# Gathering the next group's rows later: an index-driven prefetch in a mixture-of-experts kernel, moved from the start of a group to its third chunk

## The chip, the cores and the metric

One core of a Trainium2 chip. The metric is the device time of one execution in microseconds, taken as the median of several runs; lower is better. The engines are TensorE (PE, with its weight loads as PEld), VectorE (DVE), ScalarE (ACT), GpSimd (POOL) and SyncE (SP), which here only issues transfers.

## The reference

A decoder layer on 2048 rows of width 1024: a mixer (gated linear attention and retention beside each other), then a mixture of experts. The change lies in the second part:

```
logits = h @ w_router + b_router
top_val, top_idx = top_k(logits, 4)              # 4 of 32 experts for each of 2048 rows
xs = h[rows sorted by expert]
gate, up = split(ragged_dot(xs, w_gu) + b_gu)    # w_gu: 32 x 1024 x 2048
act = (clip(up, -7, 7) + 1) * min(gate, 7) * sigmoid(1.702 * min(gate, 7))
out = ragged_dot(act, w_down) + b_down           # w_down: 32 x 1024 x 1024
y[row] += weight * out                           # then residual and a last norm
```

All of it is in float32. A product is made of three passes of TensorE over operands that are split in a high and a low part (lines 119 to 121: high by high, high by low, low by high).

## The kernel before, in words

`expert_programs` writes one program for each engine, and each runs a loop over groups (`G`). The five programs meet only through semaphores. A group is one expert with one to three tiles of 128 rows and perhaps a half tile of 64 rows (slot `HALF`); an expert with more rows gets another group, which loads the expert's weights again. These inputs give 39 groups, numbered 0 to 38 here, with 70 full tiles and 9 half tiles. `G.T` is the number of full tiles, `G.U` with the half tile, `G.nT` and `G.nU` the same of the next group, `G.before` the tiles of all groups ahead.

A group has six chunks: 0 and 2 are gate columns, 1 and 3 up columns, 4 and 5 the two halves of `w_down`. Each chunk multiplies every tile with 1024x512 weights, that is 8 steps of three matmuls for a full tile and of two for a half one. In the profile's names the weights of even chunks are `weights_first`, those of odd ones `weights_split`; the rows of the tiles lie in `weights_split` as well, the activations in `tok_a_hi` and `tok_a_lo`. So "weights_first,weights_split" is chunk 0 or 2, and "tok_a_hi" marks chunks 4 and 5.

Weights come in pieces, four to a chunk, 24 to a group, of 512 KB each, in eight buffers. SyncE issues a load (L1966) when the piece eight places earlier has been split; ScalarE makes the high part (L2073) and VectorE the low part (L2173). The same two engines split the rows (L2079, L2182) and the activations (L2097, L2270).

Rows of a tile are gathered from memory into `tok_rows` by an indirect transfer from GpSimd (L1986, 512 KB for a full tile); TensorE transposes them (L2343, `rows`). A group's first tile is transposed in the chunk 4 of the group before (`next_row`, halfway through the first tile's steps), behind a wait for all gathers of the next group; its other tiles within its own chunk 0. The activations of a tile are transposed (L2351, `activations`) at the end of that tile's chunk 2 for the first half of the columns and around chunk 4 for the second. Each such transpose raises `ta_done`.

GpSimd's loop, on which the change bears, does for each group in this order:

1. wait until all rows of this group have been transposed (`tx_done`, L2023), since the gathers overwrite `tok_rows`;
2. copy the next group's row numbers to `tok_next_token` (L2026, L2028) and issue up to four gathers (L1986);
3. wait for the adds of the group before, and copy this group's row numbers and routing weights to `tok_token` and `tok_share` (L2040 to L2044);
4. for chunks 4 and 5 and each tile, wait for VectorE's weighted result (L2289, or L2277 and L2279 for a half tile) and issue its indirect add into `y_rows` (L2053).

```
with pool.If(G.nT > 0):
    pool.wait_ge(tx_done, G.before + G.U + 1)
    pool.sem_inc(wait_carrier, 1)
```

The last chunk of a group ends with TensorE waiting for `read_done` of the first tile's weighting in chunk 4, ahead of the turn of its loop.

Of the kernel before, what the change touches and what calls it, by code (L numbers as in the profile page):

```python
# [1827 lines left out]
def expert_programs(nc, k, A, keep):  # L1828
# [39 lines left out]
    def weighted_at(c, t):  # L1868

        if t == HALF:  # L1870
            return half_gu[:] if c == NGU + 1 else act_row[0:HR, HALF]
        return gu[:, 1] if c == NGU + 1 and t == 0 else act_row[:, t]
# [14 lines left out]
    def load_word(eng, g):  # L1887

        return eng.value_load(word[0:1, bass.ds(g, 1)], min_val=0, max_val=WORD - 1)
# [7 lines left out]
    def place_in(w, after=0):  # L1897
        return ((w >> 14) + after).with_bounds(min_val=0, max_val=PLACES - 1)
# [81 lines left out]
    def gpsimd(pool):  # L1980
# [4 lines left out]
        def fetch_tile(t, rows=P):  # L1985
            pool.indirect_dma_start(out=xs[0:rows, t], out_offset=None, in_=keep["h2"],  # L1986
                                    in_offset=bass.IndirectOffsetOnAxis(ap=next_token[0:rows, t:t + 1], axis=0)
                                    ).then_inc(rows_in, 16)
# [29 lines left out]
        with pool.Fori(0, NG) as g:  # L2018
            with pool.If(count > g):
                G = Group(pool, g)  # L2020
                next_word = load_word(pool, g + 1)
                with pool.If(G.nT > 0):
                    pool.wait_ge(tx_done, G.before + G.U + 1)  # L2023
                    pool.sem_inc(wait_carrier, 1)
                    place = place_in(next_word)
                    nc.gpsimd.tensor_copy(next_token[:, 0:GT], rec[:, bass.ds(place, GT), 0]).then_inc(next_set, 1)  # L2026
                    place = place_in(next_word, G.nT)
                    nc.gpsimd.tensor_copy(next_token[:, HALF:SLOTS], rec[:, bass.ds(place, 1), 0]).then_inc(next_set, 1)  # L2028
                    pool.wait_ge(next_set, g * 2 + 4)
                    pool.sem_inc(wait_carrier, 1)  # L2030
                    for t in range(GT):
                        with pool.If(G.nT > t):
                            fetch_tile(t)
                    with pool.If(G.nH > 0):
                        fetch_tile(HALF, HR)
                for half in range(2):
                    pool.wait_ge(y_out[half], G.landed(0))
                    pool.sem_inc(wait_carrier, 1)
                place = place_in(G.word)
                nc.gpsimd.tensor_copy(token[:, 0:GT], rec[:, bass.ds(place, GT), 0]).then_inc(token_set, 1)  # L2040
                nc.gpsimd.tensor_copy(share[:, 0:GT], rec[:].bitcast(F32)[:, bass.ds(place, GT), 1]).then_inc(share_set, 1)
                place = place_in(G.word, G.T)
                nc.gpsimd.tensor_copy(token[:, HALF:SLOTS], rec[:, bass.ds(place, 1), 0]).then_inc(token_set, 1)
                nc.gpsimd.tensor_copy(share[:, HALF:SLOTS], rec[:].bitcast(F32)[:, bass.ds(place, 1), 1]).then_inc(share_set, 1)  # L2044
                pool.wait_ge(token_set, g * 2 + 2)
                pool.sem_inc(wait_carrier, 1)
                for c in (NGU, NGU + 1):
                    for t in range(SLOTS):
                        with pool.If(G.has(t)):
                            rows = HR if t == HALF else P  # L2050
                            pool.wait_ge(read_done, G.chunk_tile(c, t))
                            pool.sem_inc(wait_carrier, 1)
                            pool.indirect_dma_start(  # L2053
                                out=keep["y"][c - NGU],
                                out_offset=bass.IndirectOffsetOnAxis(ap=token[0:rows, t:t + 1], axis=0),
                                in_=weighted_at(c, t), in_offset=None, compute_op=ALU.add).then_inc(y_out[c - NGU], 16)
# [377 lines left out]
    keep["expert_homes"] = xs, bias, act_row, gu, g2  # L2434
    keep["y_rows_added"] = lambda eng: field(eng, 0, TOTAL, NG * SLOTS)
    return sync, gpsimd, scalar, vector, tensor


# [183 lines left out]
```

## Time and profile before

| | |
|---|---|
| median of 3 runs | 3974.34 us (3974.16, 3974.34, 3978.67) |
| the profiled execution | 3978.82 us, its span 3976.8 us |
| PE busy | 3791.2 us, 95% of the span |
| DVE, ACT, POOL busy | 2500.3, 1614.8, 657.3 us |
| stage of the experts | from 1203 to 3925 us of the span |
| transfers | 811.29 MB, mean 204 GB/s |
| gathers of rows for the experts | 79, of them 38 groups' worth issued inside the loop |

The difference between 3978.82 and 3976.8 is what lies around the span. PE's durations overlap (a 128x512 matmul is listed at 0.39 us, and the next starts 0.227 us behind it), so a group's time is read from starts, and waits from the idle time in brackets.

### The profile page before, as it was taken

How to read it: one execution, taken by the hardware profiler on the slowest of the kernel's cores; microseconds unless marked ns; L12 is line 12 of the kernel's file. 1: busy time of each engine (PE TensorE's matmuls, PEld its weight loads, DVE VectorE, ACT ScalarE, POOL GpSimd, SP SyncE). 2: the span in 40 equal slices, each digit the busy share in tenths (PEclk: the TensorE clock that was granted, in tenths of full speed). 3: DMA queues.
4: the chain of work that ended last, by engine and by line, in shares of the span. 5: the costliest groups of instructions: out<-in, count | busy, mean ns of one | idle time of the engine just before them, and what ended most of it. 6: DMA issues, size and time to landing. Idle time of an engine off the chain costs nothing.

```text
span 3976.8 us, 67030 instructions
## 1 busy us (share of the span) xinstructions
PE 3791.2 (95%) x17917; PEld 3113.0 (78%) x17918; DVE 2500.3 (63%) x3917; ACT 1614.8 (41%) x2355; POOL 657.3 (17%) x712
## 2 busy tenths in 40 slices
PE   8999999898997999999999999999999999999995
PEld 5888788787876778878877878878888878888774
DVE  5363343696776786576577678587656565756764
ACT  3222321573223454354355454364334344433443
POOL 0110110111221211111111212122111102211301
PEclk9999999899998999999999999999999999999997
DMA  6342441664345797587588788597577566666755
GB/s 250 137 147 87 152 145 67 228 229 149 139 148 169 225 349 224 157 280 232 148 285 296 226 276 265 169 313 256 177 211 223 174 225 196 229 180 189 226 189 193
DMA packets 373240, 811.29 MB, mean 204 GB/s; under 512 B 31435, under 2 KB 31620, under 8 KB 368149
## 3 DMA queue, kind: packets, MB, share of 16 engines
q1 hardware_dynamic: 318210, 659.75, 48.1%
q0 software_dynamic: 49744, 133.33, 13.6%
q10 hardware_dynamic: 5220, 17.36, 1.1%
q8 instruction: 37, 0.61, 0.1%
q14 instruction: 29, 0.24, 0.0%
HBM read 704.36 MB, written 105.97 MB: 204 GB/s over the span
## 4 chain that ended last, share of the span: by engine, by line
PE 58%; DVE 8%; issue 5%; DMA 2%; DVEq 2%; ACT 1%; SPq 0%; POOL 0%; POOLq 0%; ACTq 0%
PE tok_bank_acc L119 15%; PE tok_bank_acc L121 15%; PE tok_bank_acc L120 15%; DVE weights_split L2173 2%; PE tok_bank_acc L2423 2%; PE tok_bank_acc L2424 2%; DVE weights_first L2173 2%; PE tok_bank_ta L2351 1%; PE rou_bank_acc L119 1%; PE rou_bank_acc L121 1%; PE rou_bank_acc L120 1%; PE tok_bank_tx L2343 1%; DMA weights_raw<-in_w_gu 1%; PE rou_bank_sm L1781 1%; DVE tok_a_lo L2270 1%
## 5 line engine op out<-in xcount | busy, mean ns | idle before, releaser
L2073 ACT CAST weights_split<-weights_raw 128x1024 fp32r<-128x1024 f32 x468 | 477.3, 1057 | 398.0 <-PE tok_bank_acc L121 271.3
L2173 DVE TENSOR_TENSOR weights_split<-weights_raw,weights_split 128x1024 fp32r<-128x1024 f32 x468 | 545.6, 1218 | 29.2 <-ACT weights_first L2073 13.9
L2173 DVE TENSOR_TENSOR weights_first<-weights_raw,weights_first 128x1024 fp32r<-128x1024 f32 x464 | 538.0, 1217 | 8.3 <-ACT weights_first L2073 8.2
L2073 ACT CAST weights_first<-weights_raw 128x1024 fp32r<-128x1024 f32 x464 | 472.7, 1051 | 141.6 <-PE tok_bank_acc L121 91.5
L2053 POOL DMA_INDIRECT y_rows<-tok_act_row,tok_token x110 | 205.8, 1871 | 1957.3 <-DVE tok_act_row L2289 1922.3
L119 PE MATMUL tok_bank_acc<-weights_first,weights_split 128*128 128x512 f32 x1120 | 448.2, 400 | 8.9 <-DVE weights_first L2173 6.4
L119 PE MATMUL tok_bank_acc<-weights_split 128*128 128x512 f32 x1120 | 439.2, 392 | 2.8 <-DVE weights_split L2173 1.6
L121 PE MATMUL tok_bank_acc<-weights_first,weights_split 128*128 128x512 f32 x1120 | 438.0, 391 | 0.0
L120 PE MATMUL tok_bank_acc<-weights_first,weights_split 128*128 128x512 f32 x1120 | 437.0, 390 | 0.0
L121 PE MATMUL tok_bank_acc<-weights_split 128*128 128x512 f32 x1120 | 436.2, 389 | 0.0
L120 PE MATMUL tok_bank_acc<-weights_split 128*128 128x512 f32 x1120 | 435.9, 389 | 0.0
L119 PE MATMUL ent_bank_acc<-ent_w_hi,ent_h_hi 128*128 128x512 f32 x896 | 356.5, 398 | 1.4 <-DVE ent_w_lo L610 1.2
L120 PE MATMUL ent_bank_acc<-ent_w_lo,ent_h_hi 128*128 128x512 f32 x896 | 351.4, 392 | 0.0
L121 PE MATMUL ent_bank_acc<-ent_w_hi,ent_h_lo 128*128 128x512 f32 x896 | 351.1, 392 | 0.0
L2097 ACT CAST tok_a_hi<-tok_bank_ta 128x512 fp32r<-128x512 f32 (+1 forms) x158 | 88.8, 562 | 452.9 <-PE tok_bank_ta L2351 452.9
L2079 ACT CAST weights_split<-tok_bank_tx 128x512 fp32r<-128x512 f32 (+1 forms) x158 | 81.2, 566 | 431.3 <-PE tok_bank_tx L2343 431.3
L119 PEld LDWEIGHTS tok_bank_acc<-weights_first,weights_split 128*128 128x128 f32 x1120 | 211.0, 188 | 53.5 <-issue 11.1
L119 PEld LDWEIGHTS tok_bank_acc<-weights_split 128*128 128x128 f32 x1120 | 210.3, 188 | 49.8 <-issue 5.6
L119 PE MATMUL tok_bank_acc<-weights_first,tok_a_hi 128*128 128x512 f32 x560 | 229.1, 409 | 20.3 <-DVE tok_a_lo L2270 12.9
L121 PEld LDWEIGHTS tok_bank_acc<-weights_first,weights_split 128*128 128x128 f32 x1120 | 210.8, 188 | 45.0
L121 PEld LDWEIGHTS tok_bank_acc<-weights_split 128*128 128x128 f32 x1120 | 210.2, 188 | 44.4
L120 PEld LDWEIGHTS tok_bank_acc<-weights_split 128*128 128x128 f32 x1120 | 210.4, 188 | 42.6
(393 smaller groups left out, 6982.9 us busy)
## 6 DMA issues: line engine op xcount, KB each, us to landing
weights_raw<-in_w_gu SPq DMA_DIRECT2D x624, 512.0 KB, 6.8
weights_raw<-in_w_down SPq DMA_DIRECT2D x312, 512.0 KB, 7.2
tok_bias<-in_b_gu SPq DMA_DIRECT2D x39, 1024.0 KB, 4.7
proj<-ent_stage SPq DMA_DIRECT2D x112, 256.0 KB, 2.0
early_w_raw<-in_w_in POOLq DMA_DIRECT2D x12, 2048.0 KB, 11.0
ent_w_ada<-in_w_ada POOLq DMA_DIRECT2D x64, 256.0 KB, 3.5
mix_late<-proj SPq DMA_DIRECT2D x48, 256.0 KB, 3.6
mod_w_ada<-in_w_ada SPq DMA_DIRECT2D x8, 1024.0 KB, 13.4
```

The source lines that it names most:

```text
L119: nc.tensor.matmul(out, act_hi, w_hi, start=first, stop=False)
L120: nc.tensor.matmul(out, act_hi, w_lo, start=False, stop=False)
L121: return nc.tensor.matmul(out, act_lo, w_hi, start=False, stop=last)
L1781: mm = nc.tensor.matmul(sm[:, 0:E], h2T[:, s], wr[:, s], start=(s == 0), stop=(s == KD - 1))
L2053: pool.indirect_dma_start(out=keep["y"][c - NGU], out_offset=bass.IndirectOffsetOnAxis(ap=token[0:rows, t:t + 1], axis=0), in_=weighted_at ...
L2073: nc.scalar.copy(whi[c % 2][:, j * SK:(j + 1) * SK], raw[:, n % RAW]).then_inc(hi_done, 1)
L2079: nc.scalar.copy(xhi[:, t, 4 * b:4 * b + 4, 0:n], tx[:, b, :, 0:n]).then_inc(xhi_done, 1)
L2097: nc.scalar.copy(ahi[:, t, 4 * q:4 * q + 4, 0:n], ta[:, :, 0:n]).then_inc(ahi_done, 1)
L2173: nc.vector.tensor_tensor(wlo[c % 2][:, rows], raw[:, n % RAW], whi[c % 2][:, rows], ALU.subtract).then_inc(lo_done, 1)
L2270: nc.vector.tensor_tensor(out, ta[:, :, 0:n], ahi[:, t, s, 0:n], ALU.subtract).then_inc(alo_done, 1)
L2423: nc.tensor.matmul(out, a_hi[:, t, s], w_hi, start=(s == 0), stop=False)
L2424: mm = nc.tensor.matmul(out, a_hi[:, t, s], w_lo, start=False, stop=(s == KD - 1))
```

## The change

GpSimd waits for one thing more before it copies the next group's row numbers: that `ta_done` has reached the transposes of this group's first tile in chunk 2. `G.pair_tile(0, 0)` is `2 * before + 2`, and `ta_done` starts at 1, so the wait opens with that very transpose.

```diff
                 with pool.If(G.nT > 0):
                     pool.wait_ge(tx_done, G.before + G.U + 1)
+
+                    pool.wait_ge(ta_done, G.pair_tile(0, 0))
                     pool.sem_inc(wait_carrier, 1)
                     place = place_in(next_word)
                     nc.gpsimd.tensor_copy(next_token[:, 0:GT], rec[:, bass.ds(place, GT), 0]).then_inc(next_set, 1)
```

The order of instructions stays the same on every engine; GpSimd has one row more. Of the kernel before, on GpSimd, from the test for a next group to the copies:

```order
L2022 COMPARE_AND_BRANCH
L2023 REGISTER_ALU x5
L2023 ISA
L2026 ISA
L2026 COPY tok_next_token<-tok_rec 128x3
L2028 ISA
L2028 COPY tok_next_token<-tok_rec 128x1
```

And of the changed kernel, whose lines are two higher from there on:

```order
L2022 COMPARE_AND_BRANCH
L2023 REGISTER_ALU x5
L2023 ISA
L2025 ISA
L2028 ISA
L2028 COPY tok_next_token<-tok_rec 128x3
L2030 ISA
L2030 COPY tok_next_token<-tok_rec 128x1
```

L2025 is the new wait. Everything that stands behind it on GpSimd, the gathers and parts 3 and 4 of the list above, waits with it.

## Rows read from the trace of the kernel before

**Rows 1.** Windows: span's stretch, us, busy us by engine, granted clock, DMA share, GB/s.
```profile
1203.00:3925.00 2722.00, 2653.25 (x12192) 2176.48 (x12193) 1801.79 (x2132) 1189.24 (x1410) 485.41 (x474) 1.00 0.70 223
```

**Rows 2.** Windows: number 5 (two tiles) and number 18 (a tile and a half tile).
```profile
1527.10:1596.80 69.70, 69.34 (x321) 57.21 (x320) 44.95 (x52) 30.83 (x36) 12.09 (x13) 1.00 0.74 234
...
2377.20:2437.80 60.60, 58.66 (x273) 48.26 (x272) 47.78 (x58) 29.45 (x36) 13.16 (x12) 1.00 0.79 238
```

**Rows 3.** Windows: numbers 3, 16, 21, 29, 37, and the sum of all ten.
```profile
1416.43:1457.35 40.92, 36.63 (x161) 28.15 (x161) 36.15 (x39) 25.65 (x29) 10.42 (x10) 1.00 1.03 372
...
2268.80:2307.48 38.68, 35.88 (x162) 28.29 (x160) 34.32 (x37) 24.34 (x27) 10.80 (x10) 1.00 0.96 331
2602.47:2640.75 38.28, 35.63 (x162) 28.35 (x160) 34.25 (x37) 25.89 (x29) 11.04 (x9) 1.00 0.92 316
...
3157.69:3197.39 39.70, 35.64 (x162) 28.31 (x160) 34.53 (x37) 24.40 (x27) 10.78 (x11) 1.00 0.91 319
3759.56:3803.33 43.77, 37.52 (x161) 29.45 (x160) 36.24 (x39) 24.66 (x28) 11.57 (x13) 0.96 0.99 333
sum 396.03, PE 360.51 PEld 283.87 DVE 350.02 ACT 250.62 POOL 104.09; mean PE 36.05 PEld 28.39 DVE 35.00 ACT 25.06 POOL 10.41
```

**Rows 4.** Waits of POOL and PE: us in total, times, longest us.
```profile
POOL tok_next_token L2026 <- PE tok_bank_tx L2343: 47.2, 9, 13.3
...
PE tok_bank_tx L2343 <- DMA tok_rows<-h_rows,tok_next_token: 6.1, 1, 6.1
```

**Rows 5.** Timeline of POOL in number 16: start us, us, instruction, [idle before it].
```profile
2273.48 0.19 POOL L2026 COPY tok_next_token<-tok_rec 128x3 int32 x1 [1.26 <-issue]
...
2275.73 1.04 POOL L1986 DMA_INDIRECT tok_rows<-h_rows,tok_next_token  x1 [0.94 <-POOL tok_next_token L2028]
2277.08 0.98 POOL L1986 DMA_INDIRECT tok_rows<-h_rows,tok_next_token  x1 [0.30 <-issue]
```

**Rows 6.** Timeline of PE in number 16 and at the start of 17.
```profile
2284.45 0.60 PE L2351 MATMUL tok_bank_ta<-keep_const,tok_act_row 128*128 128x128 f32 x4
...
2297.01 1.09 PE L2343 MATMUL tok_bank_tx<-keep_const,tok_rows 128*128 128x128 f32 x8
...
2307.47 0.49 PE L119 MATMUL tok_bank_acc<-weights_first,weights_split 128*128 128x512 f32 x1 [0.70 <-DVE weights_first L2173]
```

**Rows 7.** Timeline of PE and POOL in number 6, where POOL had to wait.
```profile
1603.82 1.04 PE L2343 MATMUL tok_bank_tx<-keep_const,tok_rows 128*128 128x128 f32 x8
...
1605.16 0.19 POOL L2026 COPY tok_next_token<-tok_rec 128x3 int32 x1 [4.12 <-PE tok_bank_tx L2343]
...
1606.43 1.02 POOL L1986 DMA_INDIRECT tok_rows<-h_rows,tok_next_token  x1 [0.96 <-POOL tok_next_token L2028]
```

**Rows 8.** Timeline of POOL in number 21.
```profile
2606.84 1.26 POOL L2026 COPY tok_next_token<-tok_rec 128x3 int32 x1 [1.08 <-issue]
...
2610.18 1.04 POOL L1986 DMA_INDIRECT tok_rows<-h_rows,tok_next_token  x1 [0.94 <-POOL tok_next_token L2028]
```

**Rows 9.** Timeline of DVE in number 16, around the activations' transposes.
```profile
2284.04 4.63 DVE L2173 TENSOR_TENSOR weights_split<-weights_raw,weights_split 128x1024 fp32r<-128x1024 f32 x4
```

**Rows 10.** Tile tok_rows in windows of numbers 16, 29 and 37 (two, three, four gathers).
```profile
DMA to landing us min/median/max: 8.2/8.5/8.9
...
DMA to landing us min/median/max: 9.2/9.8/10.1
...
L1986 POOL DMA_INDIRECT tok_rows<-h_rows,tok_next_token x4: 977/1128/1934, 3767.6 to 3771.8; - x4
...
DMA to landing us min/median/max: 8.5/9.7/11.5
```

**Rows 11.** Timeline of PE in number 18 (a tile and a half tile).
```profile
2401.05 0.60 PE L2351 MATMUL tok_bank_ta<-keep_const,tok_act_row 128*128 128x128 f32 x4
...
2418.54 1.04 PE L2343 MATMUL tok_bank_tx<-keep_const,tok_rows 128*128 128x128 f32 x8
```

**Rows 12.** Tile tok_rows over the whole stage of the experts.
```profile
DMA to landing us min/median/max: 4.0/8.2/11.5
```

## The prediction

> **What bounds the kernel now.** I read the view by windows first, over the stage of the experts and then over single groups. Of the 2722 us of that stage TensorE is busy 2653, so at most 69 us are there to win [rows 1]. They lie unevenly. A group of two tiles takes 69.70 us and TensorE works for 69.34 of them; a group of one tile and a half tile has 1.9 us idle of 60.60 [rows 2]. Neither can gain much. Groups of a single tile are another matter: there are ten (numbers 2, 3, 7, 11, 13, 16, 21, 22, 29 and 37 of 0 to 38), together 396.03 us with 360.51 of TensorE, and the core's DMA engines are busy 0.91 to 1.03 of the time at 316 to 372 GB/s [rows 3]. They need all 24 pieces of weights of 512 KB for a third of the matmuls of a three-tile group, so they are near the bound of the transfers. The length follows what else is moved: the shortest, 38.28 us, gathers one tile of rows; number 29, with three gathers, takes 39.70; number 37, with four, 43.77 [rows 3].
>
> Then the waits. GpSimd reached the gathers' first copy with the old wait still open nine times, and TensorE waited for gathered rows once in the whole stage, 6.1 us, for the first group's own rows [rows 4]. So now the gathers are always early: they cost nothing as a wait, and something as traffic.
>
> **The change, part by part.** It adds one wait on GpSimd and no work; the gathers, their two index copies, and behind them on the same in-order queue the wait for the landed adds and the four copies of tokens and shares all move with it.
>
> *Is the wait open?* Yes. Number 16 began at 2268.80 [rows 3] and its first index copy at 2273.48 [rows 5]; the transposes it will wait for end at 2284.45 + 0.60 = 2285.05 [rows 6]. The gathers move by some 12 us in one-tile groups, and by more in larger ones.
>
> *What goes.* The traffic of the gathers leaves the first chunks of one-tile groups. The most this can give is that all ten fall to the shortest length: 396.03 - 10 x 38.28 = 13.2 us, of which 37 alone is 5.5, 3 is 2.6, 29 is 1.4. Numbers 3 and 22 follow a one-tile group and begin with a gap of 0.70 us, as in the row of number 17's first matmul [rows 6], which stays: 13.2 - 1.4 = **-11.8 us**. In larger groups nothing goes, TensorE is full there.
>
> *What comes: the deadline.* The rows are needed halfway through the fifth chunk, where TensorE transposes the next group's first tile and waits for all its gathers. In number 16 that was at 2297.01 [rows 6], 11.96 us behind the end of the activations' transposes; this group is 0.40 above the shortest, and the 0.40 lies ahead of the deadline, so I take 11.56. A further 0.70 of lateness is free, since a one-tile group is followed by that gap anyway. Against it stands GpSimd's chain:
> - from the end of TensorE's transposes to the first copy 0.30 (1603.82 + 1.04 to 1605.16) [rows 7];
> - from the first copy to the first gather's issue: 1.27 with free copies [rows 7], 3.34 where both took 1.2 us (2606.84 to 2610.18) [rows 8], 2.25 where one did (2273.48 to 2275.73) [rows 5]. At the place in question VectorE has four splits of weights in a row, 2284.04 to 2288.67 [rows 9]. I take 2.25, in the middle of both, with both as ends;
> - further issues: 1.35 from the first to the second [rows 5] and 4.2 to the fourth (3767.6 to 3771.8) [rows 10]; two thirds of it, 2.8, to the third;
> - issue to landing: 8.2 to 8.9, median 8.5, for two; 9.2 to 10.1 for three; up to 11.5 with a median of 9.7 for four [rows 10]. All these were measured in one-tile groups, with the weights' queue as full as it will be later in the group.
>
> One gather (2, 21): 0.30 + 2.25 + 8.5 = 11.05, in time; 0.3 each at the upper end (12.54 - 11.56 - 0.70). Two (3, 7, 11, 13, 16, 22): 0.30 + 2.25 + 1.35 + 8.5 = 12.40, late by 0.84, 0.14 beyond the free 0.70; six groups, **+0.8**; lower end 0, upper (3.34 and 8.9) 1.63 each, 9.8. Three (29): 0.30 + 2.25 + 2.8 + 10.1 = 15.45, **+3.2**; ends 1.3 and 4.3. Four (37): 0.30 + 2.25 + 4.2 + 11.5 = 18.25, **+6.0**; ends 3.2 and 7.1.
>
> *The clock.* Number 37 has a mean granted clock of 0.96 [rows 3]: 0.04 x 43.77 = 1.75 us lost, that is 3.5 us at 1.2 GHz, behind its long idle stretches. The 1.75 stands in the 11.8, and with a six-microsecond wait in its place I expect it back: **+1.75**; ends 0 and, with number 29 too, 3.5.
>
> *Free of cost.* A group of tile and half has 2401.65 to 2418.54 = 16.9 us for the same chain [rows 11], and at most three gathers, 15.45. Larger groups have more. The four copies of tokens and shares, at most 1.2 us each, end in number 37 some 6.8 + 1.9 + 4.8 = 13.5 us behind the transposes (1.9 is the longest gather instruction [rows 10]), and VectorE wants the shares only after the rows have come, at 18. The next group's first weights will meet the gathers' traffic; a price for it I cannot read, take as nothing because eight buffers lie between a load and its use, and leave to the second rival.
>
> **The sum:** -11.8 + 0.8 + 3.2 + 6.0 + 1.75 = 0.0; from -11.8 + 1.3 + 3.2 = -7.3 up to -11.8 + 0.6 + 9.8 + 4.3 + 7.1 + 3.5 = +13.5. The profiled execution took 3978.8, so 3978.8 again for one like it. It lies 4.5 above the median of the runs (3974.2, 3974.3 and 3978.7); against that median of 3974.3 the forecast is **3974.3**.
>
> A rule that speaks against the change: GpSimd's copies take 0.19 us free [rows 7] and about 1.2 when VectorE is splitting weights [rows 5, 8], yet never longer than one such split. The Trainium skill, "SBUF — State Buffer", section "SBUF: two separate sides", has the two engines share a port pair as an exclusive lock, held for a whole instruction by a VectorE operation with two SBUF inputs, and warns that GpSimd's descriptors starve behind such work. Read strictly, GpSimd would sit out all four splits to 2288.67, 3.3 us more than a free start, and the sum would be near +20. The rows say that it slips in between two splits, so I stay with 2.25.
>
> **The rivals.**
> *Gathers in time.* If a gather lands in 4.0 us, the shortest of the stage [rows 12], even four are there (0.30 + 2.25 + 4.2 + 4.0 = 10.75 against 11.56) and the full 11.8 is won: 3962.5. The other gathers in one-tile groups speak against it, 8.2 at least [rows 10]. The Trainium skill, "DMA: Bandwidth & Descriptors", section "Anatomy of one DMA — SWDGE (gpsimd) path", gives about 2 us plus the bytes at 436 GB/s, an estimate of 3.2 us for 512 KB, with this same result; the trace disagrees, at 8.2 to 11.5, since the weights share the engines.
> *Later landing, slower.* The landing was read at the group's start; in its middle eight pieces of weights may be outstanding. If each takes 11.5 us, the longest of the stage [rows 12], one gather costs 1.8, two cost 3.1, three 4.6, four 6.0, the clock 3.5: 3.6 + 18.8 + 4.6 + 6.0 + 3.5 - 11.8 = +25, 3999. Place: TensorE's wait for the rows in the fifth chunk of all ten groups. It decides from about 1 us above the landings of [rows 10], as each microsecond is paid by eight or more groups: 8 us. For it: the engines are saturated there too. Against it: they already were when those landings were read.
> *Nothing moves the end.* The weights may arrive no earlier, because what bounds the middle of a one-tile group is the order in which buffers come free; then each deadline is also as late as now, and of 3.2 and 6.0 only 3.2 - 1.4 and 6.0 - 5.5 are paid: 0.8 + 1.8 + 0.5 = +3, 3977. The rise of 1.3 us per gather between 21, 29 and 37 speaks against it. That the wait is fulfilled when GpSimd comes to it is excluded by the 12 us above.
>
> **How the numbers follow.** Forecast 0.64, gathers in time 0.10, later landing 0.18, nothing moves 0.08. A measurement of this kernel can tell about 0.2% from no change, 7.9 us, so the line is at 3966.4 and 3982.2. The forecast's own range is 3967.0 to 3987.8, nearly all of its weight on the near side of 3982.2, with 0.60 of its 0.64; nothing moves adds 0.08 and later landing, where it comes out at under a microsecond each, 0.03: same 0.71. Gathers in time and a little of the forecast's lower tail are faster, 0.11; the remaining 0.18 is slower. The range that holds eight in ten leaves out the first rival's full gain and the upper half of the second, and goes from 3966 to 3990.
>
> **What would show it.** Right: number 37's wait for weights at its fourth and fifth chunk gone, and instead TensorE idle some 6 us ahead of the row transposes, released by the gather; the same with 3 us in 29, and under 1 us in the two-gather groups; two- and three-tile groups as long as before to 0.1 us; the landings 8 to 9 us for two. Wrong: landings of 10 or more, or one-tile groups that wait more than 2 us for two gathers (later landing); no wait at all (in time); one-tile groups as long as before chunk by chunk (nothing moves); or any two-tile group longer than 70 us, which no case here explains.

## The result, and the profile after

Slower, by little: 3984.19 us (median of 20 runs, 3978.86 to 3987.67) against 3978.62 for the kernel before in 20 runs, a ratio of 1.0016 with a 95% interval of 1.001 to 1.0022, some 6 us. One of those 20 runs of the kernel before took 4303.04 us, in a slower state, and the ratio leaves it out. The kernel before came out 4.3 us above the median of three from which the forecast was made, and that difference is none of the change's.

The profiled execution took 3981.84 us, with a span of 3980.0. The stage of the experts, from the first group's first matmul to the last group's end, went from 2719.4 to 2726.1 us: +6.7. The view by windows puts all of it into the ten one-tile groups; the others differ by 0.1 us or less each, except numbers 0 and 1, which are 0.2 longer, and in sum these differences cancel. Here are numbers 3, 7, 11, 16, 21, 29 and 37 and the sum of all ten, to be held against [rows 3]; the columns are stretch, us, busy us of PE, PEld, DVE, ACT and POOL, granted clock, DMA share, GB/s:

```profile
1413.11:1451.82 38.71, 35.27 (x160) 28.52 (x161) 36.16 (x39) 26.77 (x30) 11.08 (x10) 1.00 1.04 376
1695.11:1734.69 39.58, 36.83 (x161) 29.85 (x160) 35.40 (x38) 24.04 (x27) 10.88 (x10) 0.96 0.92 321
1977.95:2017.69 39.74, 36.78 (x162) 29.72 (x160) 35.61 (x38) 24.25 (x27) 10.87 (x10) 0.96 0.92 320
...
2266.46:2305.12 38.66, 35.50 (x162) 28.31 (x160) 34.30 (x37) 24.14 (x27) 11.45 (x10) 1.00 0.96 328
2600.08:2638.37 38.29, 35.60 (x162) 28.34 (x160) 34.25 (x37) 25.39 (x29) 8.81 (x9) 1.00 0.92 316
...
3155.11:3198.20 43.09, 37.74 (x162) 30.50 (x160) 35.97 (x38) 24.11 (x27) 11.04 (x11) 0.92 0.92 318
3760.30:3806.48 46.18, 37.60 (x161) 29.79 (x160) 36.81 (x40) 24.35 (x28) 12.05 (x13) 0.93 0.97 324
sum 402.87, PE 364.58 PEld 291.21 DVE 355.39 ACT 249.58 POOL 106.04; mean PE 36.46 PEld 29.12 DVE 35.54 ACT 24.96 POOL 10.60
```

The sum rose from 396.03 to 402.87, by 6.8. The column to look at is the clock: 0.96 in numbers 7, 11 and 13, 0.92 and 0.93 in 29 and 37, where the kernel before had one such entry. Taken times the lengths that is 3 x 1.6 + 3.4 + 3.2 = 11.4 us of clock lost, against 1.75. This product is what TensorE's clock lost, an estimate from two rounded figures; the group gets longer by it only where TensorE sets the pace. A two-tile group and a group of tile and half are as long as in [rows 2]:

```profile
1521.51:1591.16 69.65, 69.29 (x321) 57.21 (x320) 44.95 (x52) 30.81 (x36) 11.23 (x13) 1.00 0.75 234
2374.83:2435.43 60.60, 58.67 (x273) 48.26 (x272) 47.79 (x58) 29.33 (x36) 13.02 (x12) 1.00 0.79 239
```

The waits of GpSimd and TensorE (us in total, times, longest) have turned round against [rows 4]: GpSimd now waits for the new semaphore in all 38 groups, and TensorE for gathered rows nine times, once for the first group as before and eight times in the one-tile groups with two gathers or more:

```profile
POOL tok_next_token L2028 <- PE tok_bank_ta L2353: 898.7, 38, 41.3
...
PE tok_bank_tx L2345 <- DMA tok_rows<-h_rows,tok_next_token: 23.9, 9, 6.1
```

In number 7, GpSimd's timeline (start us, us, instruction, idle before it) shows the chain of the forecast. The last line gives the time to landing of its two gathers:

```profile
1711.66 0.71 POOL L2028 COPY tok_next_token<-tok_rec 128x3 int32 x1 [13.24 <-PE tok_bank_ta L2353]
1712.31 1.19 POOL L2030 COPY tok_next_token<-tok_rec 128x1 int32 x1
1714.44 1.04 POOL L1986 DMA_INDIRECT tok_rows<-h_rows,tok_next_token  x1 [0.95 <-POOL tok_next_token L2030]
1715.78 1.99 POOL L1986 DMA_INDIRECT tok_rows<-h_rows,tok_next_token  x1 [0.30 <-issue]
...
DMA to landing us min/median/max: 7.2/7.6/8.0
```

From the first copy to the first issue 2.78 us, where 2.25 was taken; a landing of 7.2 to 8.0, where 8.5 was taken. TensorE in the same group, first a line of the kernel before, then of the changed one, and its clock two microseconds at a time:

```profile
1727.82 0.66 PE L2351 MATMUL tok_bank_ta<-keep_const,tok_act_row 128*128 128x128 f32 x4 [1.51 <-DVE tok_act_row L2247]
...
1722.17 0.66 PE L2353 MATMUL tok_bank_ta<-keep_const,tok_act_row 128*128 128x128 f32 x4 [1.51 <-DVE tok_act_row L2249]
1723.93 1.82 PE L2345 MATMUL tok_bank_tx<-keep_const,tok_rows 128*128 128x128 f32 x8 [1.11 <-DMA tok_rows<-h_rows,tok_next_token]
...
1725.98 0.63 PE L120 MATMUL tok_bank_acc<-weights_first,tok_a_hi 128*128 128x512 f32 x1
1726.40 0.63 PE L121 MATMUL tok_bank_acc<-weights_first,tok_a_lo 128*128 128x512 f32 x1
```

```profile
1721.00:1723.00 2.00, 0.66 (x4) 0.42 (x4) 1.08 (x2) 0.14 (x1) 0.00 (x0) 1.00 1.04 403
1723.00:1725.00 2.00, 1.07 (x6) 1.07 (x7) 1.52 (x2) 0.45 (x1) 0.00 (x0) 0.78 1.04 386
1725.00:1727.00 2.00, 2.00 (x8) 1.71 (x7) 2.00 (x3) 1.21 (x3) 0.00 (x0) 0.50 1.06 393
1727.00:1729.00 2.00, 2.00 (x9) 1.62 (x8) 1.85 (x4) 2.00 (x3) 0.00 (x0) 0.86 1.04 419
```

Two idle stretches follow each other, 1.51 us for the activations (there before too) and 1.11 us for the rows (new), with the 0.66 us of the activations' transposes between them. Then the granted clock is at 0.50, 1.2 GHz, for some 3.4 us, in which the matmuls start 0.43 us apart and not 0.227. The row transposes took 1.82 us and not 1.09. Number 16 had the same two stretches, 1.53 and 1.48, kept its full clock, and is as long as before (38.66 us and 38.68):

```profile
2293.84 0.66 PE L2353 MATMUL tok_bank_ta<-keep_const,tok_act_row 128*128 128x128 f32 x4 [1.53 <-DVE tok_act_row L2249]
2295.98 1.09 PE L2345 MATMUL tok_bank_tx<-keep_const,tok_rows 128*128 128x128 f32 x8 [1.48 <-DMA tok_rows<-h_rows,tok_next_token]
```

The other two-gather groups waited 1.29 us (number 11), 1.07 (13) and 1.09 (22) for the rows, and number 3 waited 2.21. Number 3 kept its full clock too, and it became shorter, 38.71 us against 40.92: there the change did what it was meant to do.

### The profile page after: what moved, and what is told of

It is laid out like the page before. It is cut to its first block, busy times and chain, and to the rows that moved or that the text cites. A ratio compares the mean times of both kernels' runs of the same rounds, so it can differ in the third digit from the quotient of the medians.

```text
span 3980.0 us, 67068 instructions
## 1 busy us (share of the span) xinstructions
PE 3794.0 (95%) x17917; PEld 3119.4 (78%) x17918; DVE 2499.8 (63%) x3917; ACT 1612.5 (41%) x2355; POOL 652.9 (16%) x712
## 4 chain that ended last, share of the span: by engine, by line
PE 63%; DVE 6%; issue 4%; DMA 3%; DVEq 1%; ACT 1%; POOL 0%; POOLq 0%; SPq 0%; ACTq 0%
PE tok_bank_acc L119 17%; PE tok_bank_acc L121 16%; PE tok_bank_acc L120 16%; PE tok_bank_acc L2425 2%; PE tok_bank_acc L2426 2%; DVE weights_split L2175 2%; DMA tok_rows<-h_rows,tok_next_token 2%; PE rou_bank_acc L119 1%; PE rou_bank_acc L121 1%; PE rou_bank_acc L120 1%; PE tok_bank_ta L2353 1%; PE tok_bank_tx L2345 1%; PE rou_bank_sm L1781 1%; DVE weights_split L2184 1%; DVE tok_act_row L2291 1%
```

## The experiments

The theory from the two traces: three terms, all in one-tile groups. Lateness of the rows, mostly free of cost with two gathers; clock lost behind the longer idle stretch, the largest; and a gain from the traffic that leaves the first chunks. Rivals: the wait costs its own length and the clock nothing; or the gathers' traffic beside late weights is what costs; or larger groups take part. The edits are cuts, shown against the changed kernel unless something else is said.

**Where it lies.** The wait only where the group has one tile:

```diff
-                    pool.wait_ge(ta_done, G.pair_tile(0, 0))
+                    pool.sem_inc(wait_carrier, 1)
+                    with pool.If(G.U < 2):
+                        pool.wait_ge(ta_done, G.pair_tile(0, 0))
+                        pool.sem_inc(wait_carrier, 1)
                     pool.sem_inc(wait_carrier, 1)
```

> The new wait in groups of one tile alone (number of tiles under two). All of the change's 6.7 us lies in the ten one-tile groups by the two traces, so this is the changed kernel: +5 to +7 against the kernel before. Rival, that a part of it comes from larger groups or from the state in which they hand over the transfers: under +3.

Measured 3983.44, ratio 1.0017 (1.0008 to 1.0026). And the complement, against this last kernel:

```diff
-                    with pool.If(G.U < 2):
+                    with pool.If(G.U > 1):
```

> The new wait only in groups of more than one tile, the complement. Larger groups keep TensorE full and have 16.9 us and more from the transposes to the deadline: within 2 us of the kernel before, one-tile groups as before (43.8 us in number 37). Rival, that larger groups pay or win: more than 3 us either way.

Measured 3977.97, ratio 0.9995 (0.9986 to 1.0004). The whole of the change is in the one-tile groups; moving the gathers of the other 28 does nothing that can be measured.

In the trace of the first of these, numbers 7 and 11 stand side by side. Number 7 waited 2.17 us for the rows, number 11 1.24:

```profile
1696.49:1738.30 41.81, 38.00 (x161) 30.75 (x160) 35.97 (x38) 24.11 (x27) 11.02 (x10) 0.92 0.92 317
1981.61:2019.88 38.27, 35.37 (x162) 28.31 (x160) 34.24 (x37) 24.10 (x27) 10.78 (x10) 1.00 0.92 317
```

At the full clock a wait of 1.24 us is free: 38.27 is the shortest length of all. With 8% of its clock lost (3.3 us) the other is 3.5 longer. Its wait was 0.9 us longer as well, but number 3 of the same trace waited 2.18 us at the full clock and took 38.68.

**Does the clock hang on chance?** The changed kernel once more, for its trace.

> The changed kernel once more, for its trace: do the low-clock stretches fall in the same groups? If they hang on chance, some of numbers 3, 7, 11, 13, 16 and 22 change sides, each 1.2 to 1.7 us longer with a stretch and at 38.3 to 39.2 without, at the same wait for the rows; 29 and 37 keep theirs.

3988.16 us, just above the highest of the 20 runs. Numbers 7, 11, 13, 16 and 22:

```profile
1697.86:1737.76 39.90, 36.56 (x161) 29.69 (x160) 35.00 (x38) 24.12 (x27) 10.88 (x10) 0.96 0.93 320
1981.01:2020.93 39.92, 36.57 (x162) 29.71 (x160) 35.05 (x38) 24.24 (x27) 10.87 (x10) 0.96 0.93 317
2090.59:2132.28 41.69, 38.03 (x162) 30.57 (x161) 35.95 (x38) 24.10 (x27) 11.41 (x10) 0.92 0.96 328
2271.53:2312.93 41.40, 38.30 (x161) 30.71 (x160) 35.97 (x38) 24.20 (x27) 11.41 (x10) 0.92 0.96 329
...
2646.08:2686.17 40.09, 37.37 (x160) 29.88 (x161) 37.03 (x40) 26.39 (x29) 11.15 (x10) 0.96 1.04 373
```

Numbers 16 and 22, at the full clock in the first trace, lost some in this one; 29 lost less (0.96, 41.71 us). In 16 and 22 the wait for the rows was the same in both traces, 1.48 and 1.44 us, 1.09 and 1.06: the same program meets the same idle time and is granted the lower clock in one execution and not in the next. Numbers 7, 11 and 13 waited longer here, 1.7 to 2.0 us. The ten groups took 406.04 us.

**Cure the clock alone.** The first attempt put transposes of a constant between the activations' transposes and the wait for the rows. They stand behind four branches, one on the group's tiles and in it three, one after the other, on the number of gathers:

```diff
-                        pe.wait_ge(rows_in, (G.before + G.U + G.nU) * 16)
                         pe.wait_ge(xlo_done, (G.before + G.U) * 2 + 2)
+                        with pe.If(G.U < 2):
+                            for more, count_of in enumerate((12, 20, 20)):
+                                with pe.If(G.nU > more + 1):
+                                    for s in range(count_of):
+                                        nc.tensor.transpose(tx[:, s // 4 % 2, s % 4], ident, ident)
+                        pe.wait_ge(rows_in, (G.before + G.U + G.nU) * 16)
                         rows(0)
```

> The changed kernel, with TensorE kept busy while it waits for the gathered rows in one-tile groups: 12, 32 or 52 transposes of a constant (some 0.11 us each) where the next group has two, three or four gathers; nothing of the output changes. Theory of the clock: the wait itself costs little, and most of the loss is the five stretches at a granted clock of 0.5 that follow the idle time (23.9 us in the changed kernel against 3.4 before, so 10 us). Then the stretches in numbers 7, 11 and 13 go, number 37 and 29 keep one at most, and the time falls by 5 to 9 us against the changed kernel: between 4 below and 1 above the kernel before. Rival, the wait alone: the rows come when they come, the fillers change nothing or delay the transposes, and the time is that of the changed kernel (+6) or more.

Measured 3982.92, ratio 1.0012 (1.0003 to 1.0021): neither. The trace says why it doesn't decide: the branches alone moved the row transposes by 1.2 us in number 21, where no filler ran (its timeline has them 2.00 us behind the start of the activations' transposes, with 1.34 idle on issue, where there was no such gap). That group nonetheless stayed at 38.27, so 1.2 us of lateness is free there too. And in number 7 the fillers came after the 1.5 us of idle time and another 0.36, and the clock was already low: twelve of them took 2.81 us, where twelve take 1.47 at the full clock.

```profile
1727.16 2.81 PE L2376 MATMUL tok_bank_tx<-keep_const 128*128 128x128 f32 x12 [0.36 <-issue]
```

Numbers 7, 13 and 29 lost clock, and the ten groups took 400.88 us.

The second attempt put twelve such transposes only ahead of the activations' ones, where TensorE idles 1.5 us in any case:

```diff
                                         with pe.If(G.T < 2):
+                                            with pe.If(G.U < 2):
+                                                for f in range(12):
+                                                    nc.tensor.transpose(tx[:, f // 4 % 2, f % 4], ident, ident)
                                             activations(G, 1, t)
```

> The changed kernel with twelve transposes of a constant on TensorE in one-tile groups, now ahead of the transposes of the activations in the fifth chunk, where TensorE is idle for 1.5 us in any case (waiting for VectorE), and with no other branch on the way to the rows. They should delay nothing. If it is the sum of the two idle stretches (1.5 us for the activations, 1.3 to 6 us for the rows) that brings the clock down, the five stretches at 1.2 GHz of the changed kernel become two or none and the time falls by 3 to 8 us against it: -2 to +3 against the kernel before. If the wait for the rows alone does it, or the clock is not part of the cost, +5 to +7 as in the changed kernel.

Measured 3979.41, ratio 1.0002 (0.9993 to 1.0011), inside the clock theory's range and 4 us below `small_only`, which ran on the same chip. Its profiled execution was its slowest, 3984.55, with the clock lost in 11, 13, 29 and 37, so half a cure. The third put twelve on each side, with no branch between them and the wait:

```diff
-                                        with pe.If(G.T < 2):
+                                        with pe.If(G.half_at == 1):
                                             activations(G, 1, t)
+                                        with pe.If(G.U < 2):
+                                            for f in range(12):
+                                                nc.tensor.transpose(tx[:, f // 4 % 2, f % 4], ident, ident)
+                                            activations(G, 1, t)
+                                            for f in range(12):
+                                                nc.tensor.transpose(tx[:, f // 4 % 2, f % 4], ident, ident)
```

> The changed kernel with twelve transposes of a constant ahead of the activations' transposes in the fifth chunk of one-tile groups and twelve behind them, with no branch between them and the wait for the rows. TensorE is then busy 2.8 us of the 3 to 3.5 it idles there in two-gather groups. Clock theory: waits of 1.3 us for the rows cost nothing by themselves (two groups of earlier runs with such a wait and a full clock are 38.3 us long, as the shortest before); the six two-gather groups stay at the full clock and at 38.3 to 39.2, at most numbers 29 and 37 keep a stretch at 1.2 GHz, and the time is 4 to 7 us under the changed kernel: -2 to +2 against the kernel before. Rival (the wait costs its own length, 1.3 x 6 and more): the two-gather groups stay at 39.5 or above whatever the clock, +5 or more.

Measured 3976.93, ratio 0.9995 (0.9986 to 1.0005): the loss is gone. TensorE in number 11 (24 fillers, 0.19 us idle between), then the windows of 7, 11, 13, 16, 37 and the sum of ten:

```profile
2003.76 1.47 PE L2418 MATMUL tok_bank_tx<-keep_const 128*128 128x128 f32 x12
2005.42 0.66 PE L2353 MATMUL tok_bank_ta<-keep_const,tok_act_row 128*128 128x128 f32 x4 [0.19 <-DVE tok_act_row L2249]
2005.91 1.47 PE L2421 MATMUL tok_bank_tx<-keep_const 128*128 128x128 f32 x12
2007.40 1.09 PE L2345 MATMUL tok_bank_tx<-keep_const,tok_rows 128*128 128x128 f32 x8
```

```profile
1696.65:1735.08 38.43, 37.80 (x185) 31.08 (x184) 34.40 (x37) 24.17 (x27) 10.88 (x10) 1.00 0.92 320
1978.37:2016.66 38.29, 37.92 (x186) 31.00 (x184) 34.26 (x37) 24.21 (x27) 11.08 (x10) 1.00 0.92 319
2086.39:2125.03 38.64, 38.20 (x185) 30.95 (x184) 34.29 (x37) 24.10 (x27) 11.20 (x10) 1.00 0.96 326
2264.46:2303.81 39.35, 38.14 (x185) 30.99 (x184) 34.52 (x37) 24.10 (x27) 11.20 (x10) 1.00 0.97 328
...
3756.14:3801.84 45.70, 39.78 (x185) 32.17 (x184) 36.38 (x40) 24.54 (x28) 12.07 (x13) 0.96 0.98 321
sum 396.64, PE 382.00 PEld 311.10 DVE 350.17 ACT 248.99 POOL 105.15; mean PE 38.20 PEld 31.11 DVE 35.02 ACT 24.90 POOL 10.52
```

The rows still come late in every two-gather group. In numbers 7 and 16 TensorE waits for them behind the fillers, 0.3 and 0.9 us; in the others the fillers cover the wait, and the transposes begin 29.0 us or more into the group, where they began 28.8 or more into it in the changed kernel. No such group pays over 1.1 us. The lower clock is left in number 37 alone. The fillers are transposes. The Trainium skill, "TensorE: Matmul & The Clock Gate", section "Part 4: PE-mode transpose", says that work in transpose mode doesn't count as busy in the same way. Here 24 float32 transposes in these groups went with the loss of clock falling from 11.4 to 1.8 us, and the time by 7 us. In this kernel they did not behave like idle time, as long as they stood on both sides of the activations' transposes.

**Cure the lateness alone.** The index copies ahead of the new wait:

```diff
                     pool.wait_ge(tx_done, G.before + G.U + 1)
-
-                    pool.wait_ge(ta_done, G.pair_tile(0, 0))
                     pool.sem_inc(wait_carrier, 1)
...
                     pool.wait_ge(next_set, g * 2 + 4)
+                    pool.wait_ge(ta_done, G.pair_tile(0, 0))
```

> The changed kernel with the new wait moved behind the two index copies, so that only the gathers wait. In the changed kernel the copies and their hand-over take 2.7 to 3.1 us from the transposes to the first gather's issue in one-tile groups. Theory (lateness of the rows, and the clock behind it): the first issue comes about 2.3 us earlier, TensorE's wait in the six two-gather groups (1.0 to 1.7) goes wholly, in number 29 3.9 becomes 1.6, in number 37 6.0 becomes 3.7, and the low-clock stretches of 7, 11, 13 go: 9 to 13 us below the changed kernel, so 3 to 7 below the kernel before. Rival (the gathers' traffic beside the late weights is what costs): the traffic comes even a little earlier into the third chunk and nothing is won, +6 against the kernel before.

Measured 3974.13, ratio 0.9993 (0.9984 to 1.0002): 8 to 9 us below the changed kernel, and a mere 2.5 below the kernel before, from which it can't be told. That is a little less than was expected. The first gather issues 1.0 us behind the transposes and TensorE waits for rows three times in the ten groups (0.8, 2.3 and 3.8 us in numbers 7, 29 and 37). All three lost clock, 1.6, 1.6 and 3.6 us; the ten groups took 395.39.

**A larger dose of lateness**, in one-tile groups alone: the wait for the end of the first tile's fourth chunk:

```diff
-                    pool.wait_ge(ta_done, G.pair_tile(0, 0))
+                    pool.sem_inc(wait_carrier, 1)
+                    with pool.If(G.U < 2):
+                        pool.wait_ge(mm_done, G.chunk_tile(3, 0))
+                        pool.sem_inc(wait_carrier, 1)
```

> The wait in one-tile groups alone, and later still: for the end of the first tile's fourth chunk, 22.5 us into the group where the transposes end at 16.3. A larger dose of the same lateness: 6.2 us more in each of ten groups. With 1.3 us free in each, 5.5 us of wait in number 2 and 21, 7.2 in the six two-gather groups, 10 in 29 and 12 in 37, and one or two low-clock stretches (1.7 us each) in every group: one-tile groups of 44 to 46, 46 to 48, 51 and 54 us, some 475 in all and +75 to +90 against the kernel before. If the deadline is not what sets their length (the transfers are), under +40.

Measured 4063.32, ratio 1.0215 (1.0199 to 1.023), +85, and 485.26 us in the ten groups. Number 2 and number 29:

```profile
1373.20:1419.52 46.32, 38.49 (x162) 30.46 (x160) 37.41 (x40) 27.35 (x31) 7.99 (x10) 0.89 0.91 300
...
3221.98:3273.22 51.24, 37.69 (x162) 30.47 (x160) 36.10 (x38) 24.11 (x27) 8.37 (x11) 0.87 0.78 266
```

The waits for the rows were 5.1 and 6.2 us with one gather, 8.5 to 9.9 with two, 11.8 and 12.6 in numbers 29 and 37. So the deadline in the fifth chunk is the one that sets the length, past what is free, and the clock's share grows along: 0.86 to 0.89 in every group, 5 to 7 us each, more than the one or two stretches expected.

**What was there to win?** The kernel before, with 16 rows in each of the loop's gathers and not 128 or 64. It leaves the rest of the rows out, so its output is not the layer's; one tile of `tok_rows` is also cleared ahead of the loop, which the cut doesn't show:

```diff
-                    pool.wait_ge(ta_done, G.pair_tile(0, 0))
...
                         with pool.If(G.nT > t):
-                            fetch_tile(t)
+                            fetch_tile(t, 16)
                     with pool.If(G.nH > 0):
-                        fetch_tile(HALF, HR)
+                        fetch_tile(HALF, 16)
```

> The kernel before with 16 rows per gather in the loop and not 128 or 64, so an eighth to a quarter of the bytes and all semaphores as before; the rest of a tile keeps old rows, so later tiles are computed from other rows. It prices the gathers' traffic in the kernel before. If the differences between one-tile groups are that traffic, all ten fall to 38.3 (39.0 behind another one-tile group) and the time is 10 to 13 us below the kernel before. If they come from the bytes of the group ahead instead, number 37 stays above 41 and the gain is under 4 us.

Measured 3971.43, ratio 0.9985 (0.9976 to 0.9995): 5.3 us below the kernel before on the same chip, between the two expectations, and under half of the 11.8 that the prediction took. Numbers 3, 29 and 37 and the sum of ten:

```profile
1413.94:1453.34 39.40, 36.00 (x161) 28.14 (x160) 35.99 (x39) 25.71 (x28) 9.54 (x10) 1.00 1.03 357
...
3153.74:3192.04 38.30, 35.65 (x161) 28.29 (x160) 34.27 (x37) 24.20 (x27) 10.62 (x11) 1.00 0.91 305
3754.68:3794.86 40.18, 36.21 (x161) 28.08 (x160) 35.80 (x39) 24.61 (x28) 11.46 (x13) 1.00 0.98 322
sum 389.75, PE 360.31 PEld 283.73 DVE 349.28 ACT 249.59 POOL 100.62; mean PE 36.03 PEld 28.37 DVE 34.93 ACT 24.96 POOL 10.06
```

Number 29 fell to the shortest length as the traffic theory says. Number 37 did not: 40.18, so at most 3.6 of its excess of 5.5 were its gathers and 1.9 were not. Its clock was 0.96 before and is 1.00 here, and the trace can't part the two. Numbers 2, 3 and 22 keep 1.1 to 1.8 over the shortest as well. In all the gathers' traffic was worth 396.03 - 389.75 = 6.3 us, read from one trace of each kernel.

**Other places for the wait.** For the end of the first tile's second chunk, and the same with the copies ahead as in `copies_first`. The edit of the first:

```diff
-                    pool.wait_ge(ta_done, G.pair_tile(0, 0))
+                    pool.wait_ge(mm_done, G.chunk_tile(1, 0))
```

> The new wait set earlier: for the end of the first tile's second chunk, 10.9 us into a one-tile group, not 16.3. Lateness theory: the rows are needed at 27.8; with two gathers they land at 10.9 + 0.3 + 2.7 + 1.35 + 8 = 23, with four at 29; no waits but 1 to 2 us in number 37, no low clock but perhaps there, and if the freed traffic in the first chunks is worth something, all one-tile groups near 38.3 to 39: 5 to 10 us below the kernel before. Rival (traffic only moves, there was nothing to win): equal to the kernel before within 2 us, with number 37 still at 43 or 44 us.

> The wait for the end of the second chunk and behind the index copies, both moves together. With the first issue at 11.2 us into a one-tile group, two gathers land at 21 and four at 27: no wait for rows anywhere, and the traffic is out of the first chunk. Expected 1 us or so below the kernel with the wait at the second chunk's end alone: 3 to 5 us below the kernel before. If numbers 3, 22 and 37 are bound by the weights whatever the place of the gathers, no gain over that kernel, -2.

Measured 3974.65, ratio 0.9993 (0.9984 to 1.0002), and 3978.32, ratio 0.9998 (0.9989 to 1.0007). Neither can be told from the kernel before, and the second's expectation was missed. With the wait at the second chunk's end number 29 is at 38.27, but 3 and 37 stay at 40.45 and 42.26, with TensorE idle 2.7 and 3.4 us at the activations' transposes. In number 3 ScalarE waited 2.8 us for the landings of weights between 1436 and 1446 us, and 0.2 in the changed kernel between 1433 and 1443, so there the gathers seem to meet weights that are needed at once. Numbers 3, 22 and 37 lost clock behind that idle time, with no wait for rows at all. Why the copies ahead did not help there is open.

**Both cures**, the edits of `copies_first` and `fill_both` together:

> Both cures together: the index copies ahead of the new wait, and the transposes of a constant around the idle stretch of one-tile groups. Without lateness in the two-gather groups and with the clock held, the freed traffic should remain as a gain: the one-tile groups near 392 to 394 us in all against 396 before, number 29 at 39 to 40 and 37 at 43 to 44, at most one stretch at 1.2 GHz, and 2 to 5 us below the kernel before. If the fillers (which run in groups with no wait as well) eat it, no difference to the kernel before.

Measured 3972.64, ratio 0.9985 (0.9976 to 0.9994): 5.8 us below the kernel before on the same chip, and some 12 below the changed kernel, which ran on another. Numbers 29 and 37 and the sum:

```profile
3156.01:3194.71 38.70, 37.80 (x185) 31.10 (x184) 34.52 (x37) 24.14 (x27) 13.25 (x11) 1.00 0.92 318
3756.77:3798.03 41.26, 38.39 (x186) 30.83 (x184) 35.89 (x39) 24.50 (x28) 14.69 (x13) 1.00 0.99 332
sum 389.97, PE 380.54 PEld 309.54 DVE 349.28 ACT 249.70 POOL 115.05; mean PE 38.05 PEld 30.95 DVE 34.93 ACT 24.97 POOL 11.50
```

389.97 us, less than the 392 to 394 expected and what the kernel with hardly any gather traffic took. No group lost clock, and TensorE waited for rows only in 29 and 37, 0.6 and 1.9 us. The later place gives the 6 us once little is late beyond what is free and the clock stays up. One control was not run, the fillers in the kernel before. By the clock alone they could have given back there no more than it lost, 1.75 us in its own trace and 3.3 in that of `large_only`, whose one-tile groups are those of the kernel before.

**The clock over all traces.** Nine traces are of kernels without fillers, `chunk3_small` left aside: the kernel before, the changed one twice, `small_only`, `large_only`, `copies_first`, `small_gather`, `chunk1` and `chunk1_copies`. Their 90 one-tile groups, by TensorE's idle time in the fifth chunk:

| idle time in the fifth chunk | groups | below the full clock |
|---|---|---|
| for the activations alone, 1.0 to 1.9 us | 54 | 4 |
| for the activations alone, 2.0 to 3.4 us | 9 | 6 |
| for the activations (1.2 to 1.6 us) and then for rows, 0.8 to 2.2 us | 19 | 11 |
| the same, for rows 2.3 to 5.8 us | 8 | 8 |

With fillers on both sides (`fill_both`, `copies_fill`) it was 1 group of 20, number 37 with a wait for rows of 4.76 us. With fillers ahead alone it was 4 of 10. So the second stretch makes a low clock likely and not certain, and a single stretch of the usual length brought one four times.

## Why the prediction was wrong

The forecast was a sum of 0.0; measured is +6.8 in the trace and about +6 in the runs, a small but clear move where none was forecast. 3984.19 us lies inside the stated range and beyond the line of 3982.2 to which 0.18 was given, but it is beyond it only with the 4.3 us by which the median of three was low.

The forecast can be held against the first trace group by group, as its terms give a length for each (38.28, with 0.14 for a second gather, 0.70 behind another one-tile group, 3.2 in number 29, 6.0 + 1.75 in 37). The sum of the differences is 6.9 us: +1.2, +1.3 and +1.4 in 7, 11 and 13, and +1.6 in 29, the four groups with a low clock to which the centre gave none; +1.4 in number 2, which is 39.7 to 40.2 us long in every kernel here but `chunk3_small`; -0.4 in 3, +0.2 in 16 and 37, nothing in 21 and 22. That number 37 came out right, 46.18 against 46.03, is luck: its floor was 1.9 us too low (40.18 in `small_gather`), and with 3.2 us for the clock that leaves 2.8 for lateness where 6.0 was taken.

By its terms:

- **Which groups.** Right. The ten one-tile groups hold all of it (`small_only`, `large_only`), and the larger ones stayed to 0.1 us, but for 0.2 in numbers 0 and 1.
- **What goes, -11.8.** The step that took the shortest length as the floor of all ten was too generous. `small_gather` gave -6.3: number 2 did not fall, and at most two thirds of number 37's excess were its own gathers. The "rise of 1.3 us per gather" is no steady rise: 0.7 for each of two to number 29, and 4.1 for the fourth. Numbers 3 and 22 fell as forecast, to 38.71 and 39.11.
- **The chain on GpSimd and the landing.** Right in kind, both sizes off and against each other: 2.8 us and not 2.25 to the first issue, 7.0 to 8.4 us and not 8.5 to landing for two. TensorE waited for rows in all eight groups with two gathers or more, and in neither with one.
- **Lateness, +0.8, +3.2, +6.0.** Too high. 0.70 us was taken as free, read from the gap at the next group's start; number 11 in `small_only` and number 16 in the first trace show 1.2 to 1.4. With the clock held, the two-gather groups pay little. What lateness cost in all is known within limits. Against `small_gather`, which lost 1.6 us of clock, the changed kernel's ten groups are 13.1 us longer, and 13.1 - (11.4 - 1.6) leaves 3.3 us for lateness. `fill_both`, as late and with 1.8 us of clock lost, is 6.9 us longer than `small_gather`, all of it in 29 and 37. Both are under the 10.0 of the forecast.
- **The clock, +1.75 with an upper end of 3.5.** This is the step that failed. It allowed a low clock to 37 and at most 29, and put it at nothing for the two-gather groups without a reason. The changed kernel lost 11.4 us of clock in the first trace and, by the same reckoning, 17 in the second. A wait of 1.1 to 2.2 us in a two-gather group was rightly costed at next to nothing as a wait and wrongly at nothing as idle time: it stands 0.7 us behind another idle stretch of 1.5 us that was there already. Of 19 groups with a wait of 0.8 to 2.2 us in the traces without fillers, 11 lost clock. `fill_both` takes the clock's loss away, leaves the lateness, and returns the time to the kernel before's; its ten groups are 6.2 us shorter than the changed kernel's. Why one such group is granted the full clock and the next is not stays open.
- **The rule that speaks against the change.** The trace goes between. GpSimd again slipped in behind a split of VectorE's and did not sit out all four. But three of its four instructions were held once, the copies at 0.71 and 1.19 us against 0.19, and the second gather's instruction at 1.99 against 1.04. That is in line with the exclusive port pair of the Trainium skill, "SBUF — State Buffer", section "SBUF: two separate sides", which is held for one instruction and not for a row of them, so that +20 was more than the page says. The starved descriptors of the same section are told there of VectorE's two-port modes, not of an operation with two SBUF inputs like these splits. With the copies out of the way (`copies_first`) it was the first gather's instruction that took 2.03.
- **The rivals.** *Gathers in time* and *nothing moves* are out. *Later landing* named the right side and place with the wrong cause: the landings were shorter than before, not longer. Its sign, a wait of over 2 us for two gathers, was met once, in number 3 with 2.21, and the landings there took 7.0 to 8.0 us.

## What to carry to other kernels

A wait that ends within the slack of the next stage can still cost time through TensorE's clock, which fell here in 11 groups of 19 with waits of 0.8 to 2.2 us: cost its idle time together with the idle stretches next to it, and look at the granted clock of both traces before anything else. Before a prefetch is moved to just ahead of its use, take its preparation (index copies, hand-overs) out from behind the new wait; it is on the path then. The floor to which a group can fall is better measured by taking the traffic out than read from the shortest of its siblings; even that was no true floor here, as number 3 took 39.40 us so and 38.71 in the changed kernel.

## What the runs showed of the hardware

- The same program with the same idle time lost clock in different groups from one execution to the next (numbers 16 and 22 here), 1.6 us of clock or twice that at a time. Single executions of the changed kernel ranged over 9 us, those of the kernel before over 8 to 11 on one chip, and a single profiled one was up to 6 us off its median (`chunk1_copies`); a term of this kind needs the median of many.
- The gathers landed sooner in the middle of a one-tile group than at its start, 7.2 to 8.4 us against 8.2 to 8.9 for the two of number 16, with the transfer engines no less busy (busy share 1.04 in the 10 us from 2286, against 0.91 in the 12 us from 2274 in the kernel before). That is no rule: in the second trace the two of number 13 took 7.8 to 8.9 us in the middle. Most of this time does not hang on a gather's own bytes: in `small_gather`, with an eighth of them, the two gathers at the start of number 16 took 7.2 to 7.4 us. Over the whole stage, in the changed kernel:

```profile
DMA to landing us min/median/max: 3.7/7.0/10.5
```

- Four branches that TensorE's queue met on the way to a wait cost 1.2 us at each passing (numbers 2 and 21 in `fill`), as much as ten transposes of 128x128.
